# Index scores pair by pair inside the projection tiles of a fused transformer kernel, instead of a stage of their own

## The chip, the cores and the metric

One core of a Trainium2 chip runs the whole program. The metric is the device time in microseconds (us) of one execution, lower is better. The engines are TensorE (PE: matmuls; PEld: its weight loads), VectorE (DVE), ScalarE (ACT), GpSimd (POOL) and SyncE (SP), which issues the loads of the weights.

## The reference, cut to what matters

The program computes two models one after the other. The change lies in the first one: two layers, 528 positions (16 learned ones and 512 of the sequence), width 1024. Each layer projects the normed input into many parts. Three of them, `qi`, `ki` and `wi`, score the keys for each query (the indexer), and only the 128 best keys of a query are attended to:

```python
for l in range(DEPTH):                       # 2 layers
    n = rms_norm(h, mix_norm_g[l])
    proj = jnp.einsum("btd,de->bte", n, w_in[l])
    q, k, v, qi, ki, wi, xr, yg, cv, gt = _split_cols(proj)
    q = rotary(rms_norm(q...)); k = rotary(rms_norm(k...))
    qi = rotary(qi...)          # 8 index heads of 64
    ki = rotary(ki...)          # one of 64
    attn = dsa_attention(q, k, v, qi, ki, wi * idx_scale)
    ...
# in dsa_attention, per block of queries
logits = jnp.einsum("bqhd,bsd->bqhs", qib, ki)
iscore = jnp.einsum("bqhs,bqh->bqs", jax.nn.relu(logits), wib)
iscore = jnp.where(admiss[None], iscore, -jnp.inf)
_, sel = lax.top_k(iscore, topk)
```

Behind the projections of q and k come the projections of the convolution branch (`cv`, a gated linear unit) and of the recurrence (`xr`, `yg`), which don't need the scores.

## The kernel before, in words

All weights stream through in 548 blocks of 128 x 1024 fp32. SyncE loads a block, GpSimd splits it into a high and a low part (`whi`, L466, and `wlo`, L468) as soon as TensorE has finished the block two before it (two slots), and TensorE makes one output tile of 128 rows of it. A tile is 8 groups of products (hi with hi, hi with lo, lo with hi: L493, L494, L496), over 528 columns in two halves of 264, or over 512. Tiles go to two accumulators in turn (`acc`, slots 0 and 1), and a tile waits for `evac` of its slot: the reader of the tile two before must be done. Two more pairs of banks, `aux[0]` and `aux[1]`, take everything else.

Each engine's program is written out by hand and runs in its order, with semaphores between the engines; no scheduler moves anything. In a layer (`proj`, L594) TensorE makes 4 tiles of v, ki and wi, 3 of qi, and 10 of the phase `kq`: 2 of k (e = 0, 1) and 8 of q (e = 2 to 9). For each of the ten, ScalarE squares the tile into `tsq` (L1108), copies it with its gain into `tqg` (L1111, which frees the accumulator) and swaps its halves into `tsw` (L1114, L1115); TensorE sums the squares (`qk_sum`, L577, one tile later; for q into single columns of `aux[1]`, second bank, from column `QSUM` = 128 on); VectorE rotates it (`turn`, L1830 to L1833, with a reciprocal of 3.45 us for each of the two k tiles). Behind e = 3 ScalarE copies the transposed `wi` out of `aux[1]` (L1120, `wi_copied`).

Then comes `index(l)` (L633), a stage of its own on three engines. For each of 4 query tiles i (W = 144, 272, 400, 528 admissible keys) and each of 8 heads, TensorE multiplies 64 rows of qi with 64 rows of ki in fp32 into `aux[head % 2]`; even heads lie on rows 0 to 63, odd heads on rows 64 to 127. ScalarE takes the relu into `tsq[head % 2]` (L1141), VectorE adds it, times the head's weight, onto the score in `mask` (L1877 for the first head, L1880 for the others). TensorE may write a bank pair again when the relu two heads before is done (`ix_relu`), ScalarE may write a `tsq` again when its add is done (`ix_acc`).

Behind it TensorE makes the 16 tiles of the convolution's projections. ScalarE takes the sigmoid of the even ones (slot 0) into `csg` (L1214), VectorE multiplies the odd ones (slot 1) with it into `cu` (L1982, which frees slot 1), and after each such product runs one eighth of `choose`: the search for the 128 best scores of each query (MAX8 and MATCH_REPLACE8, L1892, L1893). In layer 0 VectorE first runs `decay_rates` (L2419 to L2438), some 32 very small operations on constants of the recurrence, with one exp of ScalarE (L1649) in between.

## Time and profile before

| | us |
|---|---|
| median of 3 runs | 3664.69 (3662.44 to 3665.59) |
| profiled execution | 3665.75 |
| its span in the trace | 3663.9 |
| TensorE busy in it | 3530.1 (96%) |
| mean granted TensorE clock | 0.976 |

The runs lie 3 us apart. The page and the answers of the trace are of the one profiled execution; all its times count from the start of its span. "Busy" of TensorE is by records of pipelined matmuls, whose ends are modelled, so they overlap: what a matmul costs is read from one start to the next. PEclk is the granted clock as a share of 2.4 GHz.

### The profile page before, as it was taken

The numbers are of one execution on the slowest core, as the hardware profiler recorded it, in microseconds if no ns is written. First come the engines' busy times: TensorE is split into PE (matmuls) and PEld (weight loads), VectorE is DVE, ScalarE is ACT, GpSimd is POOL, SyncE is SP. The second block draws the span as 40 slices with busy tenths as digits, with TensorE's granted clock in tenths as the row PEclk, the third lists the DMA queues.
The fourth block names the chain that finished last, engine by engine and source line by source line (L and its number), as shares of the span: only waits on it lengthen the run. The fifth ranks groups of instructions, "written<-read, shape, count | busy, mean of one in ns | idle before, by whom it ended". The sixth has DMA issues, their size and how long they took to land.

```text
span 3663.9 us, 49850 instructions
## 1 busy us (share of the span) xinstructions
PE 3530.1 (96%) x20100; PEld 3036.7 (83%) x20100; DVE 2347.0 (64%) x2977; ACT 988.4 (27%) x1711; POOL 2040.9 (56%) x1100
## 2 busy tenths in 40 slices
PE   7999899999999999989999999999999999999997
PEld 7899788999999879867778788877887875688886
DVE  6677898577833666788857873387336755743335
ACT  4405542222110340454231111011003444322201
POOL 4355334465666535533556776677665552466664
PEclk9799999999999989999999999999999999999999
DMA  3122111222322312211222342333235341222332
GB/s 134 51 85 78 53 47 64 72 90 94 128 90 100 109 58 76 79 54 53 75 81 93 133 146 98 103 132 135 97 103 189 142 148 63 87 97 92 103 103 69
DMA packets 96898, 348.30 MB, mean 95 GB/s; under 512 B 10848, under 2 KB 13152, under 8 KB 93664
## 3 DMA queue, kind: packets, MB, share of 16 engines
q1 hardware_dynamic: 80064, 289.44, 23.8%
q10 hardware_dynamic: 16672, 56.70, 4.1%
q8 instruction: 101, 1.65, 0.2%
q14 instruction: 61, 0.50, 0.0%
HBM read 322.32 MB, written 23.79 MB: 94 GB/s over the span
## 4 chain that ended last, share of the span: by engine, by line
PE 46%; DVE 8%; ACT 2%; issue 1%; DMA 1%; POOL 0%; ACTq 0%; DVEq 0%; POOLq 0%
PE acc L493 13%; PE acc L494 13%; PE acc L496 13%; DVE ptmp L2177 1%; PE aux L795 1%; PE acc L743 1%; PE acc L824 1%; PE aux L803 1%; DVE pcp L2177 1%; PE aux L882 0%; PE aux L714 0%; PE aux L729 0%; DMA m<-kept_m 0%; DVE fpr L1758 0%; DVE alo L1760 0%
## 5 line engine op out<-in xcount | busy, mean ns | idle before, releaser
L466 POOL TENSOR_SCALAR whi<-raw 128x1024 fp32r<-128x1024 f32 x548 | 619.2, 1130 | 1549.2 <-PE acc L496 1528.0
L468 POOL TENSOR_TENSOR wlo<-raw,whi 128x1024 fp32r<-128x1024 f32 x548 | 1421.8, 2594 | 45.7
L493 PE MATMUL acc<-nhi,whi 128*128 128x512 f32 (+1 forms) x2776 | 951.9, 351 | 26.6 <-DVE nlo L1718 15.0
L494 PE MATMUL acc<-nlo,whi 128*128 128x512 f32 (+1 forms) x2776 | 944.7, 349 | 0.0
L496 PE MATMUL acc<-nhi,wlo 128*128 128x512 f32 (+1 forms) x2776 | 866.9, 347 | 0.0
L493 PEld LDWEIGHTS acc<-nhi,whi 128*128 128x128 f32 x2776 | 524.4, 189 | 110.8 <-issue 21.5
L494 PEld LDWEIGHTS acc<-nlo,whi 128*128 128x128 f32 x2776 | 524.2, 189 | 68.9
L493 PE MATMUL acc<-bhi,whi 128*128 128x264 f32 (+1 forms) x1864 | 555.4, 314 | 13.3 <-ACT tqg L1099 5.5
L494 PE MATMUL acc<-blo,whi 128*128 128x264 f32 (+1 forms) x1864 | 543.6, 308 | 0.0
L496 PEld LDWEIGHTS acc<-nhi,wlo 128*128 128x128 f32 x2776 | 485.8, 189 | 67.2
L496 PE MATMUL acc<-bhi,wlo 128*128 128x264 f32 (+1 forms) x1864 | 448.3, 307 | 0.0
L493 PEld LDWEIGHTS acc<-bhi,whi 128*128 128x128 f32 x1864 | 355.5, 191 | 33.7 <-ACT tqg L1099 6.8
L494 PEld LDWEIGHTS acc<-blo,whi 128*128 128x128 f32 x1864 | 355.5, 191 | 15.4
L496 PEld LDWEIGHTS acc<-bhi,wlo 128*128 128x128 f32 x1864 | 304.9, 191 | 14.9
L494 PE MATMUL acc<-alo,whi 128*128 128x512 f32 (+1 forms) x880 | 300.2, 349 | 0.0
L493 PE MATMUL acc<-ahi,whi 128*128 128x512 f32 (+1 forms) x880 | 300.1, 349 | 0.0
L496 PE MATMUL acc<-ahi,wlo 128*128 128x512 f32 (+1 forms) x880 | 279.8, 351 | 0.0
L1755 DVE TENSOR_TENSOR fpr<-acc,frs 128x512 f32<-128x512 f32 (+1 forms) x88 | 61.2, 696 | 236.2 <-PE acc L496 231.2
L1760 DVE TENSOR_TENSOR alo<-fpr,ahi 128x512 fp32r<-128x512 f32 (+2 forms) x88 | 165.0, 1875 | 66.6 <-ACT ahi L1027 66.6
L1027 ACT ACTIVATE ahi<-fpr 128x512 fp32r<-128x512 f32 (+2 forms) x88 | 56.0, 636 | 559.7 <-DVE fpr L1758 559.7
L494 PEld LDWEIGHTS acc<-alo,whi 128*128 128x128 f32 x880 | 165.6, 188 | 23.5
L493 PEld LDWEIGHTS acc<-ahi,whi 128*128 128x128 f32 x880 | 165.7, 188 | 22.1
(372 smaller groups left out, 4735.8 us busy)
## 6 DMA issues: line engine op xcount, KB each, us to landing
raw<-in_w SPq DMA_DIRECT2D x548, 512.0 KB, 3.3
kept_cp<-pcp ACTq DMA_DIRECT2D x4, 1280.0 KB, 6.5
cp<-kept_cp ACTq DMA_DIRECT2D x4, 1280.0 KB, 10.0
kept_ap<-pap ACTq DMA_DIRECT2D x4, 1024.0 KB, 4.0
kept_cs<-pcs ACTq DMA_DIRECT2D x4, 1024.0 KB, 6.4
ap__144<-kept_ap ACTq DMA_DIRECT2D x4, 1024.0 KB, 6.4
cs__155<-kept_cs ACTq DMA_DIRECT2D x4, 1024.0 KB, 6.6
merge_gates<-gout ACTq DMA_DIRECT2D x16, 256.0 KB, 3.1
```

Of the source, the lines that this page charges most:

```text
L466: pool.tensor_scalar(hi, w, 1.0, 0.0, ALU.mult, ALU.add).then_inc(sem("w_hi"), 1)
L468: pool.tensor_tensor(lo, w, hi.bitcast(F32), ALU.subtract).then_inc(sem("w_split"), 1)
L493: pe.matmul(acc[s][:, f, 0:TH], hi, xh[:, f * TH:(f + 1) * TH], start=a, stop=False)
L494: pe.matmul(acc[s][:, f, 0:TH], hi, xl[:, f * TH:(f + 1) * TH], start=False, stop=False)
L496: m = pe.matmul(acc[s][:, f, 0:TH], lo, xh[:, f * TH:(f + 1) * TH], start=False, stop=z)
L743: m = pe.matmul(out, v[0:w, c, (hh // 4) * P:(hh // 4 + 1) * P], pts[0:w, c, 0:r], start=c == 0, stop=c == len(ps) - 1)
L795: pe.matmul(aux[0][:, 0, :], q2[rows, hh // 2, i * P:(i + 1) * P], k2[rows, hh // 2, :], start=True, stop=True).then_inc(sem("na_s"), 1)
L803: m = pe.transpose(aux[1][:, 0, c * P:(c + 1) * P], na_scores(j)[:, c * P:(c + 1) * P], ident[:, :])
L1027: act.activation(out[:, :, 0:T], fpr[:, 0:T].unsqueeze(1), ACT.Copy).then_inc(sem("ff_hi"), 1)
L1755: dve.tensor_tensor(halves(fpr[:, 0:T], T), accv(s1, T), rs, ALU.mult).then_inc(evac[s1], 1)
L1760: dve.tensor_tensor(lo[:, :, 0:T], fpr[:, 0:T].unsqueeze(1), hi[:, :, 0:T].bitcast(F32), ALU.subtract)\
L2177: tt = lambda o_, a, b_, op: then(dve.tensor_tensor(o_, a, b_, op))
```

## The change

The stage is dissolved. `index(l, pair)` now does one pair of heads (even and odd) of a query tile, 16 pairs in a layer, on each of the three engines, and the pairs stand inside other work:

- In TensorE's order, each q tile from e = 4 on (`IX_TILE`) is cut in the middle: four of its eight groups of products, a pair, the other four groups; then the norm sum of the tile before, then a second pair. Six tiles take pairs 0 to 11. The convolution's first two tiles are cut in the same way and take pairs 12 to 15; the norm sum of the last q tile stands ahead of pair 12.
- ScalarE's relus stand ahead of the square of the same tile (first pair) and between the copy and the swap (second pair); VectorE's adds of both pairs stand ahead of the rotation of the tile.
- The relus go to a buffer of their own, `ixr`, no longer to `tsq`.
- The widest scores (528) are cut into 264 and 264 columns instead of 512 and 16, and the column sums move to column 272 (`QSUM`), clear of them.
- ScalarE's first sigmoid (`conv_gate(l, 0)`) stands between pairs 12 and 13, its square roots of the norms (`std_q`) behind pair 15, and in layer 0 the exp of `decay_rates` behind that. VectorE's `decay_rates` stands behind pair 15's adds as before.
- The first pair waits in addition for `k_std`: `aux[0]` must have been read.

```diff
@@ constants
-QSUM = 128
+QSUM = 272
...
+IX_TILE = 4
+IX_CUT = [META + P * (i + 1) for i in range(NQT - 1)] + [T1 // 2]
...
+        ixr, o1 = at("ixr", [P, 2, T1], end_rnn_w)
@@ TensorE
+            def parted_tile(ph, i, rhs, T, between):
+
+                s, b = ph.slot(i), ph.block(i)
+                if ph.nth(i):
+                    pe.wait_ge(evac[s], ph.nth(i))
+                pe.wait_ge(sem("w_split"), b + 1)
+                products(s, b % 2, 0, KD // 2, rhs, T, True, False)
+                between()
+                products(s, b % 2, KD // 2, KD // 2, rhs, T, False, True, w0=KD // 2).then_inc(pe_block, 1)
...
                 for e in range(10):
-                    tile(kq, e, normed if e < KV else mine, T1 if e < KV else T)
+                    if e < IX_TILE:
+                        tile(kq, e, normed if e < KV else mine, T1 if e < KV else T)
+                    else:
+                        parted_tile(kq, e, mine, T, lambda: index(l, 2 * (e - IX_TILE)))
                     if e:
                         qk_sum(l, e - 1)
                     if e == 1:
                         turn_wi()
-
-            def index(l):
...
+                    if e >= IX_TILE:
+                        index(l, 2 * (e - IX_TILE) + 1)
+
+            def index(l, pair):
+
+                i = pair // (IXH // 2)
+                W, cut = META + P * (i + 1), IX_CUT[i]
+                if pair == 0:
+                    pe.wait_ge(sem("pj_done"), 15 * l + 5)
+                    pe.wait_ge(sem("wi_copied"), l + 1)
+                    pe.wait_ge(sem("k_std"), KV * (l + 1))
+                for z in range(2):
+                    it = l * NQT * IXH + 2 * pair + z
+                    if it >= 2:
+                        pe.wait_ge(sem("ix_relu"), it - 1)
+                    rows = slice(64 * z, 64 * z + 64)
+                    lhs = qi[rows, pair % (IXH // 2), META + i * P:META + (i + 1) * P]
+                    m = pe.matmul(aux[z][:, 0, 0:cut], lhs, ki[rows, 0:cut], start=True, stop=True)
+                    if W > cut:
+                        m = pe.matmul(aux[z][:, 1, 0:W - cut], lhs, ki[rows, cut:W], start=True, stop=True)
+                    m.then_inc(sem("ix_logit"), 1)
...
-                index(l)
-                for n in range(16):
-                    tile(AT[f"conv{l}"], n, R(bhi, blo, T1), T1)
+                conv, normed = AT[f"conv{l}"], R(bhi, blo, T1)
+
+                def last_sum():
+                    qk_sum(l, 9)
+                    index(l, 12)
+
+                parted_tile(conv, 0, normed, T1, last_sum)
+                index(l, 13)
+                parted_tile(conv, 1, normed, T1, lambda: index(l, 14))
+                index(l, 15)
+                for n in range(2, 16):
+                    tile(conv, n, normed, T1)
@@ ScalarE
+                for z in range(2):
+                    it = l * NQT * IXH + 2 * pair + z
+                    act.wait_ge(sem("ix_logit"), it + 1)
+                    if it >= 2:
+                        act.wait_ge(sem("ix_acc"), it - 1)
+                    if W > cut:
+                        act.activation(halves(ixr[:, z, 0:W], W), aux[z][:, :, 0:cut], ACT.Relu).then_inc(sem("ix_relu"), 1)
+                    else:
+                        act.activation(ixr[:, z, 0:W], aux[z][:, 0, 0:W], ACT.Relu).then_inc(sem("ix_relu"), 1)
...
-                index(l)
+                index(l, 12)
+                conv_gate(l, 0)
+                for pair in range(13, 16):
+                    index(l, pair)
+                std_q(l)
                 if l == 0:
                     act.wait_ge(sem("lam_abs"), 1)
                     act.activation(prep[:, 1, :], prep[:, 0, :], ACT.Exp, scale=-1.0).then_inc(sem("lam_exp"), 1)
-                conv_gates(l)
+                for n in range(1, KD):
+                    conv_gate(l, n)
@@ VectorE
                 for e in range(HEADS):
+                    if KV + e >= IX_TILE:
+                        index(l, 2 * (KV + e - IX_TILE))
+                        index(l, 2 * (KV + e - IX_TILE) + 1)
                     turn(7 + e, q[:, e, LO[l]:], LT[l], LO[l], 0)
...
-                index(l)
+                for pair in range(12, 16):
+                    index(l, pair)
+                dve.wait_ge(sem("ix_acc"), (l + 1) * NQT * IXH)
                 if l == 0:
                     decay_rates()
                 conv_inputs(l)
```

How it moves instructions. TensorE's row in layer 0 before, from the end of the last q tile (`acc`) through the norm sums (`aux<-ones,tsq`) into the stage of index scores (`aux<-ki,qi`, a count for the heads):

```order
L493 MATMUL acc<-bhi,whi 128x264
L494 MATMUL acc<-blo,whi 128x264
L496 MATMUL acc<-bhi,wlo 128x264 x2
L589 MATMUL aux<-ones,tsq 128x1 x4
L589 MATMUL aux<-ones,tsq 16x1
L644 MATMUL aux<-ki,qi 128x144 x2
L589 MATMUL aux<-ones,tsq 128x1 x4
L589 MATMUL aux<-ones,tsq 16x1
L644 MATMUL aux<-ki,qi 128x144 x6
L644 MATMUL aux<-ki,qi 128x272 x8
L644 MATMUL aux<-ki,qi 128x400 x8
L644 MATMUL aux<-ki,qi 128x512
```

TensorE's row now, in the middle of the first cut q tile (e = 4), around pair 0:

```order
L498 MATMUL acc<-blo,whi 128x264
L500 MATMUL acc<-bhi,wlo 128x264 x2
L666 MATMUL aux<-ki,qi 128x144 x2
L497 MATMUL acc<-bhi,whi 128x264
L498 MATMUL acc<-blo,whi 128x264
```

and at that tile's end, around the norm sum and pair 1:

```order
L500 MATMUL acc<-bhi,wlo 128x264 x2
L603 MATMUL aux<-ones,tsq 128x1 x4
L603 MATMUL aux<-ones,tsq 16x1
L666 MATMUL aux<-ki,qi 128x144 x2
L497 MATMUL acc<-bhi,whi 128x264
```

The run of score matmuls is gone; two heads at a time stand between products that don't need them.

VectorE's row before, at the end of the last rotation (`q<-tqg,tsw`) in layer 0: all adds in a run, then `decay_rates` (`prep`).

```order
L1830 TENSOR_TENSOR tqg<-tqg,rope 128x528
L1831 TENSOR_TENSOR tsw<-tsw,rope 128x528
L1833 TENSOR_TENSOR q<-tqg,tsw 128x528
L1877 TENSOR_SCALAR mask<-tsq,wi 128x144
L1880 SCALAR_TENSOR_TENSOR mask<-tsq,wi,mask 128x144 x7
L1877 TENSOR_SCALAR mask<-tsq,wi 128x272
L1880 SCALAR_TENSOR_TENSOR mask<-tsq,wi,mask 128x272 x7
L1877 TENSOR_SCALAR mask<-tsq,wi 128x400
L1880 SCALAR_TENSOR_TENSOR mask<-tsq,wi,mask 128x400 x7
L1877 TENSOR_SCALAR mask<-tsq,wi 128x528
L1880 SCALAR_TENSOR_TENSOR mask<-tsq,wi,mask 128x528 x7
L2419 COPY prep<-par 128x8 x2
```

VectorE's row now, at the same place:

```order
L1920 SCALAR_TENSOR_TENSOR mask<-ixr,wi,mask 128x400 x4
L1867 TENSOR_TENSOR tqg<-tqg,rope 128x528
L1868 TENSOR_TENSOR tsw<-tsw,rope 128x528
L1870 TENSOR_TENSOR q<-tqg,tsw 128x528
L1917 TENSOR_SCALAR mask<-ixr,wi 128x528
L1920 SCALAR_TENSOR_TENSOR mask<-ixr,wi,mask 128x528 x7
L2458 COPY prep<-par 128x8 x2
```

Four adds (two pairs) stand ahead of each rotation, and only the adds of the widest query tile are left between the last rotation and `decay_rates`. They now wait for pairs that TensorE makes inside and behind the convolution's first two tiles.

## Rows read from the trace of the kernel before

**Rows 1.** The page's part 1: busy time, share of the span, instructions.
```profile
PE 3530.1 (96%) x20100; PEld 3036.7 (83%) x20100; DVE 2347.0 (64%) x2977; ACT 988.4 (27%) x1711; POOL 2040.9 (56%) x1100
```
**Rows 2.** By stretch: length, busy time of each engine (instructions), PEclk, DMA share, GB/s.
```profile
101.34:143.16 41.82, 41.82 (x350) 41.60 (x348) 23.99 (x23) 15.44 (x26) 21.47 (x13) 1.00 0.24 76
143.16:178.99 35.83, 31.91 (x93) 21.06 (x91) 18.80 (x33) 14.71 (x34) 2.64 (x2) 0.53 0.05 15
178.99:182.67 3.68, 3.68 (x17) 3.68 (x17) 2.83 (x9) 3.04 (x7) 0.00 (x0) 0.50 0.01 2
...
1302.66:1341.50 38.84, 38.84 (x194) 32.49 (x193) 24.50 (x23) 15.00 (x26) 21.40 (x13) 1.00 0.25 82
1341.51:1377.43 35.92, 31.88 (x90) 21.06 (x89) 18.82 (x33) 14.83 (x34) 2.77 (x2) 0.52 0.05 15
1377.43:1380.75 3.32, 3.32 (x16) 3.32 (x16) 1.60 (x3) 2.09 (x4) 0.00 (x0) 0.50 0.02 5
```
**Rows 3.** TensorE's timeline, score stage: start, length, line, tiles, count [idle <-releaser].
```profile
143.16 0.52 PE L644 MATMUL aux<-ki,qi 64*128 64x144 f32 x4
143.61 1.19 PE L589 MATMUL aux<-ones,tsq 128*128 128x1 f32 x10
...
173.23 2.57 PE L644 MATMUL aux<-ki,qi 64*128 64x512 f32 x4 [0.20 <-ACT tsq L1141]
```
**Rows 4.** TensorE's timeline at full clock: fp32 sums of squares, a tile's start.
```profile
86.30 1.05 PE L583 MATMUL aux<-tsq,ones 128*128 128x264 f32 x4
...
87.65 0.39 PE L493 MATMUL acc<-bhi,whi 128*128 128x264 f32 x1
87.88 0.28 PE L494 MATMUL acc<-blo,whi 128*128 128x264 f32 x1
```
**Rows 5.** ScalarE's timeline around the copy of wi, in layer 0 and in layer 1.
```profile
104.70 0.70 ACT L1111 ACTIVATE tqg<-acc,par 128x528 f32<-128x528 f32 x1 [3.56 <-DVE k L1838]
...
106.76 0.20 ACT L1120 ACTIVATE wi<-aux 128x32 f32<-128x32 f32 x1
...
1308.26 0.20 ACT L1120 ACTIVATE wi<-aux 128x32 f32<-128x32 f32 x1
```
**Rows 6.** Groups by shape, 143 to 180 us: busy, mean ns | idle before.
```profile
L1880 DVE SCALAR_TENSOR_TENSOR mask<-tsq,wi,mask 128x528 f32<-128x528 f32 x6 | 4.6, 768 | 4.7 <-ACT tsq L1141 4.4
L1141 ACT ACTIVATE tsq<-aux 128x528 f32<-128x528 f32 x8 | 4.5, 608 | 7.6 <-PE aux L646 7.6
```
**Rows 7.** Timelines of VectorE and of GpSimd behind a q tile's end.
```profile
137.95 1.58 DVE L1830 TENSOR_TENSOR tqg<-tqg,rope 128x528 f32<-128x528 f32 x1 [3.91 <-ACT tsw L1115]
139.56 0.71 DVE L1831 TENSOR_TENSOR tsw<-tsw,rope 128x528 f32<-128x528 f32 x1
...
136.57 2.40 POOL L468 TENSOR_TENSOR wlo<-raw,whi 128x1024 fp32r<-128x1024 f32 x1
```
**Rows 8.** VectorE's timeline: decay_rates of layer 0 and the first product cu.
```profile
180.91 0.38 DVE L2419 COPY prep<-par 128x8 f32<-128x8 f32 x2
...
186.67 3.74 DVE L2436 TENSOR_SCALAR hba<-par 128x8 f32<-128x8 f32 x4
...
192.72 0.71 DVE L1982 TENSOR_TENSOR cu<-acc,csg 128x528 f32<-128x528 f32 x1 [1.88 <-issue]
```
**Rows 9.** ScalarE's timeline and a stretch (columns as in rows 2) of the convolution.
```profile
210.28 0.61 ACT L1214 ACTIVATE csg<-acc 128x528 f32<-128x528 f32 x1 [11.13 <-PE acc L496]
...
200.00:240.00 40.00, 40.00 (x329) 40.00 (x328) 32.08 (x87) 1.84 (x3) 23.06 (x14) 1.00 0.28 92
```
**Rows 10.** TensorE alone: two waits, each with its slow stretch: length, busy, PEclk, DMA.
```profile
292.47:294.51 2.04, 0.01 (x2) 1.00 0.19 76
295.30:298.70 3.40, 3.40 (x12) 0.50 0.27 82
...
1588.95:1595.29 6.34, 0.00 (x1) 0.77 0.18 55
1592.40:1599.20 6.80, 3.91 (x9) 0.50 0.24 80
```

More of the change, by code:

```diff
@@ L1104, in proj @@
                     T = T1 if e < KV else LT[l]
+                    if e >= IX_TILE:
+                        index(l, 2 * (e - IX_TILE))
                     block_done(kq.block(e) + 1)
@@ L1112, in proj @@
                        .then_inc(evac[s], 1)
+                    if e >= IX_TILE:
+                        index(l, 2 * (e - IX_TILE) + 1)
                     act.wait_ge(evac[s], kq.nth(e) + 1)
@@ L1128, in std_q, with index @@
                 act.activation(qstd[:, 0:NQT], sums[:, 0:NQT], ACT.Sqrt, bias=EPS, scale=1.0 / HD).then_inc(sem("q_std"), 1)
-            def index(l):
-                for i in range(NQT):
-                    W = META + P * (i + 1)
-                    for hh in range(IXH):
-                        it = (l * NQT + i) * IXH + hh
-                        act.wait_ge(sem("ix_logit"), it + 1)
-                        if hh >= 2 or i:
-                            act.wait_ge(sem("ix_acc"), it - 1)
-                        src = aux[hh % 2][:, :, :].rearrange("p a b -> p (a b)")[:, 0:W]
-                        if it == l * NQT * IXH:
-                            act.wait_ge(sem("qk_sum"), 10 * (l + 1))
-                        act.activation(tsq[:, hh % 2, 0:W], src, ACT.Relu).then_inc(sem("ix_relu"), 1)
-                std_q(l)
+            def index(l, pair):
+                i = pair // (IXH // 2)
+                W, cut = META + P * (i + 1), IX_CUT[i]
+                for z in range(2):
[7 more added lines that the diff above has]
+                        act.activation(ixr[:, z, 0:W], aux[z][:, 0, 0:W], ACT.Relu).then_inc(sem("ix_relu"), 1)
             def exps(l, j):
@@ L1206, in rnn, with conv_gate @@
                 part(7)
-            def conv_gates(l):
+            def conv_gate(l, n):
                 ph = AT[f"conv{l}"]
-                for n in range(KD):
-                    block_done(ph.block(2 * n) + 1)
-                    if n:
-                        act.wait_ge(evac[1], ph.nth(2 * n - 1) + 1)
-                    act.activation(halves(csg[:, :], T1), accv(0, T1), ACT.Sigmoid).then_inc(evac[0], 1)
+                block_done(ph.block(2 * n) + 1)
+                if n:
+                    act.wait_ge(evac[1], ph.nth(2 * n - 1) + 1)
+                act.activation(halves(csg[:, :], T1), accv(0, T1), ACT.Sigmoid).then_inc(evac[0], 1)
             def att_split(l):
@@ L1865, in query_scales, with index @@
                 then(dve.reciprocal(qrs[:, 0:NQT], qstd[:, 0:NQT]))
-            def index(l):
-                dve.wait_ge(sem("wi_copied"), l + 1)
-                for i in range(NQT):
-                    W = META + P * (i + 1)
-                    sc = mask[:, i, 0:W]
-                    for hh in range(IXH):
-                        it = (l * NQT + i) * IXH + hh
-                        r, w = tsq[:, hh % 2, 0:W], wi[:, i, hh:hh + 1]
-                        dve.wait_ge(sem("ix_relu"), it + 1)
-                        if hh == 0:
-                            dve.tensor_scalar(sc, r, w, None, ALU.mult).then_inc(sem("ix_acc"), 1)
-                        else:
-                            dve.wait_ge(sem("ix_acc"), it)
-                            dve.scalar_tensor_tensor(sc, r, w, sc, ALU.mult, ALU.add).then_inc(sem("ix_acc"), 1)
-                dve.wait_ge(sem("ix_acc"), (l + 1) * NQT * IXH)
+            def index(l, pair):
+                i = pair // (IXH // 2)
+                sc = mask[:, i, 0:META + P * (i + 1)]
+                if pair == 0:
+                    dve.wait_ge(sem("wi_copied"), l + 1)
+                for z in range(2):
+                    it, hh = l * NQT * IXH + 2 * pair + z, 2 * (pair % (IXH // 2)) + z
+                    r, w = ixr[:, z, 0:META + P * (i + 1)], wi[:, i, hh:hh + 1]
+                    dve.wait_ge(sem("ix_relu"), it + 1)
+                    if hh == 0:
+                        dve.tensor_scalar(sc, r, w, None, ALU.mult).then_inc(sem("ix_acc"), 1)
+                    else:
+                        dve.wait_ge(sem("ix_acc"), it)
+                        dve.scalar_tensor_tensor(sc, r, w, sc, ALU.mult, ALU.add).then_inc(sem("ix_acc"), 1)
             def choose(l, n):
```

18 lines of the change are left out of this document (2 added, 16 removed).

## Prediction

> **What bounds the kernel now.** I read the page's busy shares first: TensorE matmuls are busy for 3530.1 of 3663.9 us, VectorE for 64%, ScalarE for 27% [rows 1]. TensorE is the path nearly everywhere, so a change is worth what it takes out of TensorE's own row of work, waits and slow clock. The table by stage shows where the change works. The index scores of the first layer fill 35.83 us and those of the second 35.92 us, at a mean granted clock of 0.53 and 0.52; the query projections ahead of them run at 1.00 [rows 2]. The clock also stays at its lower level (0.50, that is 1.2 of 2.4 GHz) for the first 3.68 and 3.32 us of the convolution's first tile [rows 2]. TensorE's timeline shows why the stage is long. The first pair of heads, still at full clock, is over in 0.45 us (143.16 to 143.61); later pairs each wait for ScalarE's relu of the pair before, and one of the widest keeps TensorE for 2.57 us at half clock [rows 3]. It is a loop of matmul, relu and weighted add with nothing beside it.
>
> **What is taken out.** From 143.16 to 178.99 is 35.83 us, in which one norm sum of 1.1 us stays (it moves into the convolution's first tile): 34.7 us go. The slow head of the convolution, 3.68 us at half rate, did 1.84 us of work, so 1.8 us more go. Layer 0: 36.5 us. Layer 1: 35.92 - 1.0 + 1.66 = 36.6 us. Together **73.1 us**.
>
> **What is put in: 16 pairs of matmuls a layer, in TensorE's row.** The two heads of a pair stand on different halves of the rows and run side by side. At full clock four fp32 matmuls of 264 columns take 1.05 us with the tail of the last [rows 4], 0.22 to 0.24 each, so four of 512 columns at half clock would take 3.7 us one after the other; they took 2.57 [rows 3], so they overlap. So a pair of 144 columns costs 0.45 us (seen), 272 columns 2 x 0.23 + 0.1 = 0.56, 400 columns 2 x 0.34 + 0.1 = 0.78, and 528 columns, now cut 264 and 264, 4 x 0.22 + 0.1 = 1.0; four of each make 11.2 us. A tile that starts again after such a group loses 0.11 us (first matmul 0.23 us to the next [rows 4] instead of the 0.12 that a tile of 5.87 us [rows 9] gives each of its 48), 16 times: 1.8 us. That is 13.0 us a layer, **26.0 us** in all. From below it is bounded by the columns alone, some 10 us a layer. From above, each way in and out of the two-halves arrangement could cost the tail of a matmul: a record lasts 0.28 us where the next starts after 0.12 [rows 4, 9], so 0.16 us, 32 times, 5.1 us instead of the 1.8.
>
> On this the Trainium skill has a rule that speaks against the change: "TensorEngine Tiling (Array Packing)", section Key Properties, says that changing the tiling mode drains TensorE. In the row at 143.16 the norm sum behind the pair starts 0.45 us after the pair did, which leaves no room for a full drain beside the work; by the rule taken at its worst the sum would be that of the rival "drains" below.
>
> **Waits that the change adds.** Three.
>
> (a) The first pair needs wi, the weights of the heads, which ScalarE copies at 106.76 to 106.96, held up by the key's rotation on VectorE (its copy at 104.70 waited 3.56 us for k) [rows 5]. Nothing ahead of that point is changed. TensorE begins the tile at 101.34 [rows 2] and would reach the pair half a tile (2.98 us) later, at 104.3, and wait until 107.05: **2.7 us**. In layer 1 it is 1302.66 + 2.84 = 1305.50 against 1308.5: **3.0 us** [rows 2, 5]. Before, the copy had 36 us of cover.
>
> (b) Pair on pair. TensorE's next pair needs the relus of the last one, about 3.1 us later in its row (half a tile, or half a tile and a norm sum). The widest relu takes 0.61 us, the widest add 0.77 [rows 6]. But VectorE's adds now meet GpSimd, which in the old stage stood idle. A VectorE operation with two SBUF operands that starts during one of GpSimd's splits of the weights lasts until that is over: the rotation at 137.95 took 1.58 us instead of 0.71, ending when the split that began at 136.57 did [rows 7]. The Trainium skill says the same ("SBUF — State Buffer", the exclusive lock on the shared port pair); the trace agrees. After the change the second pair of each tile is added from the split's end, 3.65 us behind the tile's end. VectorE's work in a tile is then the wait of about 2.1 us, four adds of 1.7 to 2.7 us and the rotation of 2.2 us, at most 7.0 of the tile's 8.1 to 8.8 us. The relus are done 1.8 to 2.4 us before TensorE wants them: **0 us**, and ScalarE (27% busy, one or two table loads more, each while it waits anyway) hides the rest.
>
> (c) The accumulator of the convolution's second tile. Call T the end of that tile on TensorE. The last pair follows it, its relus end at T + 1.8, its first add meets the split (T + 0.1 to T + 3.7) and ends at T + 4.4, the second at T + 5.2. In layer 0 VectorE has decay_rates next: from 180.91 to 190.84, 9.9 us, with 3.0 us of stops for GpSimd in it (four small constants take 3.74 us instead of 0.7, where GpSimd splits the weights behind the first tile) [rows 8]. It meets the next split again, begun at T + 7.0, so it is over at T + 15.2. Only then comes the product cu, 0.71 us, which frees the accumulator (evac1): T + 16.1. TensorE has the pair (1.1 us) and tile 2 (5.87 us: two tiles lie between ScalarE's sigmoids, 11.13 + 0.61 [rows 9]) and wants the accumulator for tile 3 at T + 7.0. It waits **9.1 us**. In the old order this work lay under the first two tiles and ended 1.88 us before cu could run [rows 8], so it was free; the change takes the cover. Bounds: without meeting GpSimd 4.9 us, with two more stops 11.5 us. In layer 1 there is no decay_rates: cu ends at T + 6.0, before 7.0, **0 us**. From then on VectorE catches up: it is busy for 32.08 of 40 us there, 9.4 of the 11.74 us of two tiles [rows 9]; the end of the convolution and the recurrence behind it see it as before.
>
> **The clock.** A wait of TensorE of 2.04 us is followed by 3.4 us at 0.50; one of 6.34 us lowers the clock within it, 6.8 us long and 3.9 us past its end [rows 10]. Work done in those stretches takes twice as long: 1.7 us lost behind each wait of (a) (none, if the clock holds), 2.0 us behind (c) if the same 3.9 us fall behind it, 3.4 if all 6.8 do, say 2.8. Together **6.2 us**. In the tiles with pairs I expect 1.00.
>
> **Sum.** 73.1 - 26.0 - 5.7 - 9.1 - 6.2 = **26.1 us**: some 7 in layer 0 and 19 in layer 1. The profiled execution took 3665.75 us (span 3663.9), 1.06 above the median of the three runs, 3664.69. So 3639.6 for a profiled execution, and **3638.6** as a median.
>
> **Rivals.**
> - Light stall: the adds and decay_rates slip between the splits and the clock stays up behind the short waits. (c) is 4.9 us and the clock costs 2 us: 8.4 us less, 3630. For: the meeting times are worked out, not seen. Against: operations as small as the constants did stop [rows 8].
> - Drains: the dearer boundary, 5.1 us a layer instead of 1.8, 6.6 us more, 3645. For: the rule of the page. Against: the seen 0.45 us.
> - Deep stall: decay_rates stops at a second split, or the low clock behind it stretches tile 3 so that tile 5 waits too: 2.4 + 4 us, 3645 to 3651.
> - Pair by pair: the old loop comes back inside the tiles, each pair waiting for the relu before it, whose add waits for GpSimd. It decides once the margin of about 2 us is used up; at 0.8 us lost at each of 32 pairs the gain is gone, 3664.
> - Slower: the half clock comes with the pairs themselves. The old stage was at 0.53, with TensorE's records nearly continuous [rows 2, 3]; if the fp32 matmuls on half of the rows hold the clock down rather than the gaps between them, the eight tiles that now hold pairs, about 47 us a layer, run at half: 94 us more, 3733. It decides from 52 us of low clock in all (half of it is 26). Against: the clock was still full in the first pair and fell only once the waits had begun.
>
> **Chances.** The forecast 0.66, its own range 3632 to 3645; light stall 0.13; drains and deep stall 0.12; pair by pair 0.04; slower 0.05. The range of 8 in 10 takes the forecast, most of the light stall and most of the two dear cases: 3628 to 3649. A measurement of this kernel tells 0.2%, 7.3 us, from no change. Faster by more: 0.91; within: 0.03; slower by more: 0.06.
>
> **What would show it.** Right: no stretch of index scores alone; TensorE's granted clock near 1.00 from the fourth query tile to the convolution's second but for some 3.4 us behind two waits for wi; one wait of about 9 us for cu ahead of the convolution's fourth tile in layer 0, none there in layer 1; layer 1 gaining over twice what layer 0 does; VectorE's add behind each tile's end at 1.8 to 2.6 us instead of 0.4 to 0.8. Wrong: waits of TensorE for ixr relus (pair by pair), a granted clock of 0.5 across the q tiles, pairs of 400 columns that take over 1 us at full clock, or no wait ahead of the fourth tile.

## The result and the profile after

The changed kernel takes 3640.18 us (median of 4 runs, 3638.83 to 3640.98), the kernel before 3664.24 beside it (4 runs). The ratio is 0.9934, with a 95% interval of 0.992 to 0.9947: 24.1 us faster. The profiled execution took 3640.31 us with a span of 3638.2, 25.7 under the span before. Of these 25.7, 1.7 us arise ahead of the first changed matmul, where the kernels are the same, in part by a stretch at half clock near 57 us that only the profiled execution before had (its clock is 0.72 from 56 to 62 us, after it is 1.00).

The page's part 1 of the changed kernel answers to [rows 1]: TensorE's busy time fell from 3530.1 to 3496.3 us. Part of that is no work saved: the same matmuls are shorter at the upper clock.

```profile
PE 3496.3 (96%) x20100; PEld 3005.5 (83%) x20100; DVE 2357.7 (65%) x2977; ACT 991.6 (27%) x1715; POOL 2039.8 (56%) x1100
```

By stretch, TensorE alone (length, busy time with its instructions, granted clock, DMA share, GB/s), against [rows 2]: in each layer from the start of kq tile 4, the first with a pair in it, until behind the last pair; then the slow stretches of layer 0 in them (layer 1 has one, 3.4 us from 1300.6).

```profile
99.60:178.46 78.86, 76.35 (x584) 0.98 0.18 61
1293.44:1367.10 73.66, 70.81 (x402) 0.98 0.17 58
...
105.88:109.29 3.41, 3.41 (x16) 0.51 0.00 0
181.00:191.20 10.20, 4.16 (x19) 0.50 0.13 51
```

No stretch of scores at 0.53 is left; the tiles with the pairs in them run at 0.98, and what is missing to 1.00 is one stretch of 3.4 us behind the first pair in each layer. (The first stretch holds the convolution's third tile too, which ends at 178.46, where the long stop begins; the last pair ends at 172.34. In layer 1 it ends at 1364.10, 3 us ahead of the end of the stretch.)

TensorE's timeline (start, length, line, tiles, count, idle before) shows a pair of each width, with the tile's matmul that follows, and the one long stop:

```profile
105.31 0.52 PE L666 MATMUL aux<-ki,qi 64*128 64x144 f32 x4 [2.51 <-DVE q L1870]
...
122.92 0.73 PE L666 MATMUL aux<-ki,qi 64*128 64x272 f32 x4
123.58 0.39 PE L497 MATMUL acc<-bhi,whi 128*128 128x264 f32 x1
123.81 0.28 PE L498 MATMUL acc<-blo,whi 128*128 128x264 f32 x1
...
139.85 0.94 PE L666 MATMUL aux<-ki,qi 64*128 64x400 f32 x4
...
158.56 0.72 PE L666 MATMUL aux<-ki,qi 64*128 64x264 f32 x4
159.11 0.62 PE L668 MATMUL aux<-ki,qi 64*128 64x264 f32 x4
159.66 0.39 PE L497 MATMUL acc<-bhi,whi 128*128 128x264 f32 x1
...
187.04 0.59 PE L497 MATMUL acc<-bhi,whi 128*128 128x264 f32 x1 [8.58 <-DVE cu L2021]
```

From a pair's first matmul to the tile's next it is 0.44, 0.66, 0.88 and 1.10 us, and the tile's first matmul takes 0.23 to its next (123.58 to 123.81). Ahead of a pair in the middle of a tile 0.09 us are lost too: the last matmul of the half takes 0.21 to the pair instead of 0.12. The pair of 144 columns costs what the very first one cost in [rows 3], at full clock, and no pair but the first of a layer waits.

ScalarE's timeline, against [rows 5]: the copy of wi (L1153) comes 1.75 us earlier than before, as the tile itself does (the 1.7 us from above), and TensorE's first pair starts 0.1 us behind it. TensorE's row names q as releaser; the copy is the last thing that the pair needed, as the first experiment shows.

```profile
102.95 0.70 ACT L1142 ACTIVATE tqg<-acc,par 128x528 f32<-128x528 f32 x1 [3.56 <-DVE k L1875]
...
105.01 0.20 ACT L1153 ACTIVATE wi<-aux 128x32 f32<-128x32 f32 x1
```

VectorE's timeline from the last pairs of layer 0 to the product cu, against [rows 6 to 8], and below it GpSimd's, with the splits of the weights beside it:

```profile
168.85 1.64 DVE L1920 SCALAR_TENSOR_TENSOR mask<-ixr,wi,mask 128x528 f32<-128x528 f32 x2 [0.94 <-ACT ixr L1173]
173.08 3.29 DVE L1920 SCALAR_TENSOR_TENSOR mask<-ixr,wi,mask 128x528 f32<-128x528 f32 x2 [2.59 <-ACT ixr L1173]
176.41 0.38 DVE L2458 COPY prep<-par 128x8 f32<-128x8 f32 x2
...
178.61 1.01 DVE L2468 TENSOR_TENSOR prep<-prep 128x16 f32<-128x16 f32 x1
...
179.86 2.19 DVE L2468 TENSOR_TENSOR prep<-prep 128x16 f32<-128x16 f32 x1
...
186.28 0.71 DVE L2021 TENSOR_TENSOR cu<-acc,csg 128x528 f32<-128x528 f32 x1
```

```profile
172.53 2.40 POOL L472 TENSOR_TENSOR wlo<-raw,whi 128x1024 fp32r<-128x1024 f32 x1
...
178.55 1.05 POOL L470 TENSOR_SCALAR whi<-raw 128x1024 fp32r<-128x1024 f32 x1 [3.62 <-PE acc L500]
179.68 2.34 POOL L472 TENSOR_TENSOR wlo<-raw,whi 128x1024 fp32r<-128x1024 f32 x1
```

The adds of the last pair, of which the first starts during the split at 172.53, take 3.29 us together and not the 1.64 of the pair before. The first ends at 175.50, 0.56 us behind the split: it stood until the split was over and then still had most of its own work to do. Then come the decay rates, 9.8 us, with two more stops, 1.01 and 2.19 us for an operation of 0.17, which end with GpSimd's two operations at 178.55 and 179.68. Only then comes cu.

### The profile page after: what moved, and what is told of

Same layout as the page of the kernel before. It is cut to its first block, busy times and chain, and to the rows that moved or that the text cites. A ratio compares the mean times of both kernels' runs of the same rounds, so it can differ in the third digit from the quotient of the medians.

```text
span 3638.2 us, 49855 instructions
## 1 busy us (share of the span) xinstructions
PE 3496.3 (96%) x20100; PEld 3005.5 (83%) x20100; DVE 2357.7 (65%) x2977; ACT 991.6 (27%) x1715; POOL 2039.8 (56%) x1100
## 4 chain that ended last, share of the span: by engine, by line
PE 46%; DVE 8%; ACT 2%; issue 1%; DMA 1%; POOL 0%; ACTq 0%; DVEq 0%; POOLq 0%
PE acc L497 14%; PE acc L500 13%; PE acc L498 13%; DVE ptmp L2216 1%; PE aux L815 1%; PE acc L763 1%; PE acc L844 1%; PE aux L823 1%; ACT us L1550 1%; DVE pcp L2216 1%; DVE ru L1978 0%; PE aux L734 0%; PE aux L749 0%; PE aux L902 0%; DMA m<-kept_m 0%
## 5 line engine op out<-in xcount | busy, mean ns | idle before, releaser
L497 PE MATMUL acc<-bhi,whi 128*128 128x264 f32 (+1 forms) x1864 | 556.8, 315 | 24.9 <-DVE cu L2021 8.6
L497 PEld LDWEIGHTS acc<-bhi,whi 128*128 128x128 f32 x1864 | 355.2, 191 | 57.1 <-issue 10.2
L498 PEld LDWEIGHTS acc<-blo,whi 128*128 128x128 f32 x1864 | 354.9, 190 | 14.9
L1086 ACT ACTIVATE fsq<-h 128x528 f32<-128x528 f32 x56 | 36.2, 646 | 546.6 <-DVE h L1824 332.1
```

The lines of the kernel that those rows point to most:

```text
L497: pe.matmul(acc[s][:, f, 0:TH], hi, xh[:, f * TH:(f + 1) * TH], start=a, stop=False)
L498: pe.matmul(acc[s][:, f, 0:TH], hi, xl[:, f * TH:(f + 1) * TH], start=False, stop=False)
```

## The experiments

The theory: the gain is the stage that is gone, with its waits and its half clock; what is lost of it are three waits, each the price of one position in a queue, and the slow stretches behind them. Rivals: that the buffers carry the gain, that boundaries or the order of the matmuls matter, or that the waits have other causes. All comparisons are with 3640.2 for the changed kernel; the kernel before stood at 3664.7 to 3665.3 beside these runs, against 3664.2, so that some 0.5 to 1 us of such a difference is not the kernel's.

### The copy of wi one tile earlier

```
-                    if e == 3:
+                    if e == 2:
                         act.wait_ge(sem("wi_turned"), l + 1)
```

> One edit to the changed kernel: ScalarE copies the turned score weights (wi) behind the swap of q/k tile 2 instead of tile 3, in both layers. Nothing is left out. My theory: in the profile of the changed kernel TensorE stood for 2.5 us (102.80 to 105.31) and 2.85 us (1296.48 to 1299.33) before the first pair, because the copy of wi came to the head of ScalarE's queue late; each stop was followed by a stretch of 3.4 us at half clock, worth 1.7 us each. With the copy a tile earlier both stops and both slow stretches go: 2.5 + 2.85 + 3.4 = 8.8 us, so about 3631.4 us beside 3640.2 of the changed kernel. Rival A: the first pair's start is held by something else as well (its tile, the adds), and only a part comes back: 0 to 4 us, 3636 to 3640. Rival B: the slow stretches are not due to the stops but come up anyway somewhere near: 5.4 us, 3634.8.

Measured: 3632.46 us (5 runs), ratio to before 0.9913 (0.99 to 0.9927); 7.7 us less than the changed kernel. TensorE's timeline and ScalarE's:

```profile
103.71 0.52 PE L666 MATMUL aux<-ki,qi 64*128 64x144 f32 x4
```

```profile
103.94 0.70 ACT L1142 ACTIVATE tqg<-acc,par 128x528 f32<-128x528 f32 x1 [3.56 <-DVE k L1875]
```

The first pair starts without a wait, at 103.71, before ScalarE's evacuation of the tile behind which the copy stood, at 103.94. The slow stretches behind the pairs are gone in both layers. So the wait was the copy's place in the queue. But a smaller one takes its place, at the third pair. TensorE's rows of it in both layers, and the relu of the second pair that it waits for:

```profile
111.82 0.98 PE L666 MATMUL aux<-ki,qi 64*128 64x144 f32 x4
...
1302.21 0.98 PE L666 MATMUL aux<-ki,qi 64*128 64x144 f32 x4 [0.54 <-ACT ixr L1175]
```

```profile
111.47 0.29 ACT L1175 ACTIVATE ixr<-aux 128x144 f32<-128x144 f32 x1 [2.89 <-DVE mask L1917]
```

That pair keeps TensorE for 0.91 us instead of 0.45, in layer 1 behind a wait of 0.54. The relu stood for the first add, which came late on VectorE. In the changed kernel the long wait for wi had hidden this. It is 0.5 us in layer 0 and 1.0 in layer 1, and so most of what is missing to the 8.8 us expected: by the traces layer 0 gained 3.6 us and layer 1 3.4.

### The decay rates spread among the pairs' adds

```
                     if KV + e >= IX_TILE:
                         index(l, 2 * (KV + e - IX_TILE))
+                        if l == 0 and KV + e != IX_TILE + 1:
+                            next(rates, None)
                         index(l, 2 * (KV + e - IX_TILE) + 1)
...
-                if l == 0:
-                    decay_rates()
```

> One edit to the changed kernel: the decay rates of layer 0 (VectorE's work between the last pair's adds and the layer's first evacuation of a convolution tile) are cut in six pieces and put between the two pairs' adds of the query tiles 4 and 6 to 9, the last piece ahead of pair 13; ScalarE's exp for them goes ahead to tile 5. Nothing is left out. My theory: the stop of 8.6 us in layer 0 (178.46 to 187.04, TensorE waiting for VectorE's evacuation of a convolution tile) is caused by the decay rates standing in VectorE's queue at 176.4 to 186.2, and the half clock of 10.2 us from 181.0 by that stop; 7 us of those 10.2 lie within the stop and about 4 us of it behind, worth about 2.1 us. With the rates spread: 8.6 + 2.1 = 10.7 us less, about 3629.5 us beside 3640.2. Rival A: the stop has another cause, which the queue's order only hides (ScalarE's square, a queue of evacuations behind the pairs): it shrinks only by a part, 3634 to 3640. Rival B: the pieces delay the adds of the pairs, and through the two buffers the next pair's matmuls: small stops at 5 tiles come instead, and 3 to 5 us of the gain are given back, 3633 to 3635.

Measured: 3625.28 us (4 runs), ratio 0.9889 (0.9874 to 0.9904); 14.9 us less. VectorE's timeline: an operation of one of the pieces, and cu behind the last adds.

```profile
136.11 1.03 DVE L2473 TENSOR_SCALAR prep<-prep 128x16 f32<-128x16 f32 x1
...
173.83 3.29 DVE L1922 SCALAR_TENSOR_TENSOR mask<-ixr,wi,mask 128x528 f32<-128x528 f32 x2 [2.59 <-ACT ixr L1176]
...
177.28 0.71 DVE L2023 TENSOR_TENSOR cu<-acc,csg 128x528 f32<-128x528 f32 x1
```

The same operations, the stop at 136.11 too, now cost TensorE nothing: cu starts 0.2 us behind the last add, and no wait for it is left. Matmul by matmul, the traces of the two kernels move apart by 10.7 us around 187 us, the 8.6 of the wait and 2.1 of clock that the theory had. That the time fell by 4 us more has its largest part, 2.4 us, some 1270 us later, in layer 1, where the edit changes nothing. TensorE's wait for the first taps there, in the changed kernel (us in total, times, longest):

```profile
PE aux L685 <- DVE ru L1978: 4.5, 1, 4.5
```

With the rates spread the same wait is 2.1 us long (1454.33 to 1456.40). The reason shows in VectorE's three taps and GpSimd's split, first of the changed kernel, then of the kernel with both edits (below), where the wait is 2.1 us as well:

```profile
1463.21 5.10 DVE L1978 SCALAR_TENSOR_TENSOR ru<-rx,par,ru 128x528 f32<-128x528 f32 x3
```

```profile
1465.08 2.67 POOL L472 TENSOR_TENSOR wlo<-raw,whi 128x1024 fp32r<-128x1024 f32 x1
```

```profile
1445.24 3.03 DVE L1980 SCALAR_TENSOR_TENSOR ru<-rx,par,ru 128x528 f32<-128x528 f32 x3
```

```profile
1447.80 2.69 POOL L472 TENSOR_TENSOR wlo<-raw,whi 128x1024 fp32r<-128x1024 f32 x1
```

Where the split starts 1.9 us behind the first of the three taps, they take 5.10 us; where it starts 2.6 us behind, 3.03. The third tap decides: it starts at 1465.58, 0.5 us behind the split's start, and takes 2.73 us, or at 1446.85, 0.95 us ahead of it, and takes 1.42. A shift of 0.7 us between two engines is worth 2.1 us to VectorE and 2.4 to TensorE. These 2.4 us are luck, not an effect of the spread rates as such; they are in the result of the kernel with both edits too. With the copy of wi alone moved the wait was 4.5 us as before; what makes the shift was not tested.

### Both

> The two edits together (wi copied one tile earlier, the decay rates spread among the pairs' adds). Nothing is left out. My theory, by which the two stops are separate mechanisms that add: 8.8 + 10.7 = 19.5 us, about 3620.7 us beside 3640.2 of the changed kernel. Rival: time saved on TensorE's queue in the projections is taken back by a later wait (the gates' stops of 2.05 and 4.5 us at 283 and 1464 us grow by it, or those of a DMA), so that the two together give less than the sum of the two apart: 3624 to 3632.

Measured: 3618.2 us (4 runs), ratio 0.9873 (0.9858 to 0.9888); 22.0 us less than the changed kernel, where the two edits gave 7.7 and 14.9 alone. The two waits are separate causes and add up. The third pair still loses the 0.5 and 1.0 us of the first experiment, and the 2.4 us at the taps of the second are in the 22.0, so that the two moves by themselves gave some 19.6, beside 19.5 expected. (In the trace the taps' wait of layer 1 is 2.1 us long.) From 98 to 170 us, the stretch of the pairs in layer 0, the granted clock is 1.00 (and so it is in layer 1):

```profile
98.00:170.00 72.00, 72.00 (x561) 1.00 0.18 62
```

### The stage kept, with the new buffers and cuts

```
-                        parted_tile(kq, e, mine, T, lambda: index(l, 2 * (e - IX_TILE)))
+                    tile(kq, e, normed if e < KV else mine, T1 if e < KV else T)
...
+                for pair in range(16):
+                    index(l, pair)
+                    if pair == 0:
+                        qk_sum(l, 9)
+                for n in range(16):
                     tile(conv, n, normed, T1)
```

> One part of the change alone: the buffers of their own for the relus and the cuts of the rows are kept as in the changed kernel, but the 16 pairs of each layer stand again in a stage of their own behind the last query projection, and the tiles are whole. Nothing is left out. My theory is that the gain comes from the place alone: in a stage of their own each pair waits for relu and adds, whatever the buffers. Then the time is that of the kernel before within 3 us: about 3662 us (3659 to 3667). Rival: the buffers of their own carry a good part of the gain, since relu and adds no longer exclude each other there: 8 us or more of the 24 come with the stage kept, 3656 us or less.

Measured: 3662.93 us (10 runs), ratio 0.9993 (0.9983 to 1.0002), not to be told from before. The stretch of the scores in layer 0, all engines in the columns of [rows 2]:

```profile
144.84:180.60 35.76, 31.77 (x91) 19.36 (x92) 20.53 (x37) 15.33 (x36) 1.22 (x1) 0.52 0.04 16
```

Own buffers without the new place give nothing: the stage has its old length and its old clock.

### Both pairs behind the tile

```
-                        parted_tile(kq, e, mine, T, lambda: index(l, 2 * (e - IX_TILE)))
+                        tile(kq, e, mine, T)
...
+                        index(l, 2 * (e - IX_TILE))
                         index(l, 2 * (e - IX_TILE) + 1)
```

> One part of the change undone: the eight tiles that had a pair in their middle are whole again, and both pairs stand one behind the other at the tile's end (ScalarE and VectorE take them in the same order). Nothing is left out. My theory: a pair directly behind a pair must wait for the relus of the first, whose buffers in the banks it overwrites. From the first pair's end that is a relu of 0.5 to 0.8 us for each half and its hand-overs, so 0.5 to 1.0 us of waiting at each of the 16 second pairs, 8 to 16 us in all; against it stand the mid-tile restarts of TensorE that go, 16 times 0.1 to 0.2 us. About 3649 us beside 3640.2 of the changed kernel (3644 to 3656). Rival: the relu is ready within the run of matmuls of the same pair, the stops are hidden, and only the restarts go: 3637 to 3640.

Measured: 3650.94 us (7 runs), ratio 0.9963 (0.9951 to 0.9974); 10.8 us more than the changed kernel. TensorE's timeline at a pair behind a pair:

```profile
125.11 0.73 PE L667 MATMUL aux<-ki,qi 64*128 64x272 f32 x4
126.32 1.01 PE L667 MATMUL aux<-ki,qi 64*128 64x272 f32 x4 [0.48 <-ACT ixr L1177]
```

The second pair waits for the relu of the first, and its two heads start apart, since each waits for its own: two pairs take 2.15 us instead of 2 x 0.66. Over the widths it is 0.6, 0.8, 1.05 and 1.2 us, twice each in a layer: some 15 us, less the mid-tile restarts (3 to 4 us), and a stretch at the lower clock comes back in each layer (0.70 from 156.5 to 160, 0.83 from 1330 to 1340). So 3 us of tile between two pairs are worth more than the restart that they cost.

### The scores twice, head by head and by turns

```
+                    for _ in range(2):
+                        m = pe.matmul(aux[z][:, 0, 0:cut], lhs, ki[rows, 0:cut], start=True, stop=True)
```

> Each score matmul of the changed kernel is issued twice in a row, into the same place with the same operands, so that the output stays the same; nothing is left out. This prices the pairs' matmuls by themselves where they now stand. My theory of the sum: they cost 11.2 us a layer (22.4 in both) at full clock and the restarts around them 1.8 us a layer; the second issue adds the first part alone: about 22 us, 3662 us beside 3640.2. Rival A: the boundaries between the pairs and the tile (TensorE changing from 128 rows to 64 and back) are the dear part and the matmuls of the two row halves overlap: less than 16 us more, under 3656. Rival B: the longer pairs delay the relus and adds and make new stops: over 26 us more, above 3666.

Measured: 3662.65 us (10 runs), ratio 0.9993 (0.9984 to 1.0003); 22.5 us more. The number is the theory's, its parts are not. Doubled pairs of 144, 272 and 400 columns take 0.70, 1.12 and 1.55 us (0.25, 0.46 and 0.68 more), those of 528 columns 2.97, 1.87 more instead of 0.88:

```profile
163.99 0.71 PE L667 MATMUL aux<-ki,qi 64*128 64x264 f32 x2
164.54 0.61 PE L669 MATMUL aux<-ki,qi 64*128 64x264 f32 x2
164.98 0.72 PE L667 MATMUL aux<-ki,qi 64*128 64x264 f32 x4
165.43 0.71 PE L669 MATMUL aux<-ki,qi 64*128 64x264 f32 x4
165.98 0.60 PE L667 MATMUL aux<-ki,qi 64*128 64x264 f32 x2
166.43 0.61 PE L669 MATMUL aux<-ki,qi 64*128 64x264 f32 x2
166.96 0.39 PE L497 MATMUL acc<-bhi,whi 128*128 128x264 f32 x1
```

The first four records are one head alone, the middle eight both, the last four the other alone. By the widths the doubling costs TensorE some 26 us in the two layers, and 1.3 us of that come back in the wait for cu (7.3 us). The rest of the difference to 22.5 was not traced, so that the hit on 22 is in part luck. The order was then tested by itself:

```
-                for z in range(2):
+                for n in range(4):
+                    z = n % 2
```

> Each score matmul again twice, the same work as in the run with the scores doubled, but the two heads take turns: head 0, head 1, head 0, head 1 instead of twice head 0 and then twice head 1. Nothing is left out. In that run a doubled pair of 144, 272 and 400 columns took 0.25, 0.46 and 0.68 us more than a single one, as two heads side by side do; a pair of 528 columns took 1.87 us more instead of 0.88, and the second head's matmuls began beside the first's only when the first had four records left. Theory A: the heads go side by side only if the second's matmuls stand at most some four records behind the first's in TensorE's queue; by turns they do, and the widest pairs fall to 0.88 us more each, 8 x 0.99 = 7.9 us less than 3662.7: about 3655 us. Rival: the widest pairs are limited by something else (two banks written at a time); the order changes nothing, 3661 to 3664.

Measured: 3654.76 us (7 runs), ratio 0.9973 (0.9962 to 0.9985); 7.9 us less. TensorE's timeline of the same pair:

```profile
164.16 0.72 PE L667 MATMUL aux<-ki,qi 64*128 64x264 f32 x4
164.71 0.62 PE L669 MATMUL aux<-ki,qi 64*128 64x264 f32 x4
165.15 0.71 PE L667 MATMUL aux<-ki,qi 64*128 64x264 f32 x4
165.59 0.72 PE L669 MATMUL aux<-ki,qi 64*128 64x264 f32 x4
166.24 0.39 PE L497 MATMUL acc<-bhi,whi 128*128 128x264 f32 x1
```

The widest pairs fall to 2.08 us, from 2.97, eight times 0.89: 7.1 of the 7.9 us. It was the order in the queue.

### One relu buffer

```
-                    if it >= 2:
-                        act.wait_ge(sem("ix_acc"), it - 1)
+                    if it >= 1:
+                        act.wait_ge(sem("ix_acc"), it)
...
+                        act.activation(halves(ixr[:, 0, 0:W], W), aux[z][:, :, 0:cut], ACT.Relu).then_inc(sem("ix_relu"), 1)
```

> The changed kernel with one of the two relu buffers alone: both relus of a pair write the same one, so that the second waits for the first's add, and each pair's first relu for the last pair's second add. Nothing is left out. My theory: inside the tiles a pair has 5.8 us until the next, and relu, add, relu, add take about 3.5 us in a row, 5.1 us where the first add stands still for GpSimd's split; so nothing of it reaches TensorE but perhaps at the pairs behind the tiles' ends of layer 0's last two tiles: 0 to 1 us, 3640 to 3641 us. Rival: ScalarE's evacuation of the query tile stands behind the second relu and comes late for TensorE's next tile but one: 1 us at each of 12 tiles, 3650 us or more.

Measured: 3640.23 us (4 runs), ratio 0.9932 (0.9916 to 0.9949): the same as with two. In the trace one pair of each layer is late by most of a microsecond, though. In layer 0, ScalarE's timeline and TensorE's:

```profile
168.19 0.61 ACT L1173 ACTIVATE ixr<-aux 128x528 f32<-128x528 f32 x1 [2.42 <-DVE mask L1920]
```

```profile
168.05 0.71 PE L666 MATMUL aux<-ki,qi 64*128 64x264 f32 x2
...
168.86 0.71 PE L666 MATMUL aux<-ki,qi 64*128 64x264 f32 x2
```

The relu of the pair before stood 2.42 us for an add that GpSimd's split held up, and the second head of pair 14 could start only behind that relu, at 168.86: 1.89 us instead of 1.10, and the wait for cu became 9.6 us. Layer 1 shows 2.08 us at the same pair, and five earlier pairs there are late by 0.05 to 0.31. In the runs this does not show, and where the traces win it back was not looked into. With two buffers TensorE came to the next pair 2.4 us or more after the first relu of the last one was over; with one buffer the 2.4 us of an add's stop are enough to use that up.

### Cuts of 512 and 16

```
-IX_CUT = [META + P * (i + 1) for i in range(NQT - 1)] + [T1 // 2]
+IX_CUT = [META + P * (i + 1) for i in range(NQT - 1)] + [512]
```

> One part of the change undone: the rows of 528 columns are cut 512 and 16 again, as in the kernel before, instead of 264 and 264, in the eight widest pairs; relu reads the two banks as one row. Nothing is left out. My theory: the columns are the same and the number of matmuls too, so TensorE's row is the same to 0.1 us a pair: 3640.2 with 1 us to either side. Rival: a matmul of 16 columns costs far more than its columns, as the sums of one column do, 0.12 us each, and with two of them per head 0.2 us a pair come on top, 2 us: 3642.

Measured: 3641.04 us (4 runs), ratio 0.9936 (0.9919 to 0.9952). A pair of 528 columns takes 1.19 us instead of 1.10, eight times 0.09: 0.7 us. The even cut is worth that much at most.

### Both, and the first taps ahead of the choice's end

```
                 taps(0)
+                for _ in rest_of_mask:
+                    pass
+                dve.sem_inc(sem("mask_done"), 1)
```

> The two edits that were tried together (wi copied a tile earlier, decay rates spread) and a third: the last round of the top-k choice of the last row block and the mask's end (3.4 us of VectorE's work in each layer) go behind the first taps of the recurrent branch, which TensorE's first gates wait for. Nothing is left out. My theory: the stops of TensorE before the gates, 2.0 and 2.1 us in that kernel, go, since VectorE has 3.5 us of idle time right behind those taps: 4.1 us less than 3618.2, about 3614. Rival A: the taps are bound by the evacuation of their own tile and not by the choice before them: only 0.2 to 1 us of each stop goes, 3617 us. Rival B: GpSimd's work, which lies differently beside the taps, holds them by 2 us or more as in layer 1 of the changed kernel (4.5 us there): no gain, 3618 to 3621.

Measured: 3613.67 us (4 runs), ratio 0.9863 (0.9847 to 0.988); 4.5 us less than both edits without it, and the fastest kernel here, 26.5 us under the changed one. VectorE's timeline in layer 1, and what TensorE still waits for there:

```profile
1438.36 4.38 DVE L1983 SCALAR_TENSOR_TENSOR ru<-rx,par,ru 128x528 f32<-128x528 f32 x3
```

```profile
PE aux L685 <- DVE ru L1983: 0.6, 1, 0.6
```

The taps meet a split in this order (4.38 us), and it costs only 0.6 us, since they start earlier. In layer 0 no wait is left there. The 0.5 us at the third pair of layer 1 stay.

## Why the prediction was right

It said 3638.6 (3628 to 3649); the result is 3640.2. The terms, in the order of its sum, with what the trace of the changed kernel and the runs give:

- **Taken out, 73.1.** The stage is gone. The kernel with the stage put back is as slow as the one before. With the measured terms below the 36.5 and 36.6 give the measured gain of each layer to 0.3 us: 36.5 - 13.9 - 2.5 - 8.6 - 3.8 = 7.7 against 7.6, and 36.6 - 14.5 - 2.85 - 1.7 = 17.55 against 17.3.
- **Put in, 26.0; measured 28.4.** This is the term that was too small. From the start of kq tile 4 to the end of the last pair, without the wait for wi and the 1.7 us of its slow stretch, TensorE takes 172.34 - 99.60 - 2.5 - 1.7 = 68.5 us in layer 0 against 54.7 for the same tiles and the norm sum before (41.82 + 1.1 + 2 x 5.87 [rows 2, 3, 9]), so 13.9 for the pairs, and 66.1 against 51.6 in layer 1, 14.5. What was mis-sized is the pair of 272 columns and more: 0.1 us was added to the columns for start and boundary, and it is 0.2 (0.66, 0.88, 1.10 where 0.56, 0.78 and 1.0 stood; only 0.45 was seen). That makes 12.3 a layer for 11.2. The restarts came near their 1.8 us (1.6 and 2.2 are left for them), but not as they were counted, 16 times 0.11: a tile that starts behind a norm sum takes 0.23 us to its second matmul anyway [rows 4], so only the nine pairs a layer that stand straight behind a tile's matmuls cost one, 0.09 us ahead and 0.11 behind each. The columns alone, priced by the scores doubled by turns, are 9.4 us a layer, so that starts, changes and restarts together cost 4.5 and 5.1. The rival "drains" put 16.3 us a layer, which the 13.9 and 14.5 do not reach; whether TensorE drains in part at a change is not shown, and the 0.2 us beside the columns leave room for it.
- **(a) The wait for wi, 2.7 and 3.0; measured 2.51 and 2.85.** With the copy earlier the wait is gone; 0.5 and 1.0 us come in its place at the third pair.
- **(b) Pair on pair, 0; measured 0.** An add behind a tile's end takes 2.4 us, as said. The relus are done at least 2.4 us before TensorE wants them, where 1.8 to 2.4 was said. That the margin comes from the 3 us of tile between two pairs is shown by the kernel with the tiles uncut (10.8 us dearer). One reading in this step was wrong: the rotation at 137.95 did not end with the split (138.97), but 0.56 us later, at 139.53 [rows 7]. The times of (c) held all the same, since there an add's own time was put behind the split's end (T + 4.4; it ended at T + 4.3).
- **(c) The wait for cu, 9.1; measured 8.58**, with the decay rates as its cause, since it goes when they are spread. None in layer 1. From the second tile's end, T = 171.2, the rates begin at T + 5.2 as forecast and cu is over at T + 15.8 (16.1 forecast); TensorE wants the accumulator at T + 7.2 (7.0). The 3.0 us of stops in the rates came as two, 0.8 and 2.0, in other operations than before.
- **The clock, 6.2; measured 5.5.** 3.4 us at 0.50 behind each wait of (a), and 10.2 us from 181.0 around (c), of which 4.2 lie behind it and cost 2.1, where 2.8 was taken. The rival "slower", by which the matmuls on half of the rows hold the clock down, is refuted: the clock is 1.00 in all tiles with pairs once the waits are gone, and the stage put back runs at 0.52 with the same matmuls.

The sum with these numbers is 73.1 - 28.4 - 5.4 - 8.6 - 5.5 = 25.2 us. That the forecast came so near has some luck in it: the pairs cost 2.4 us more than said, the waits and the clock 1.5 us less. The mechanism, each wait with its place and its size, was as forecast. The traces show it by layer: from kq tile 4 to the first gates of the recurrence layer 0 gained 7.6 us (7 forecast) and layer 1 17.3 (19 forecast), 24.9 together, and the medians differ by 24.1 us. The 7.6 of layer 0 is a near hit by the same offset; in layer 1 the dearer pairs show. The light stall was refuted by the two stops in the decay rates (8.58 us and not 4.9), the deep one since no further tile waits.

What the prediction did not ask is how cheaply the three waits could be had back: three small groups of instructions moved in the queues of ScalarE and VectorE gave another 22.0 us beside the 24.1, of which 2.4 are the lucky taps of layer 1.

## What to carry to other kernels

A loop of small steps between engines costs TensorE its waits and then its clock; the same matmuls put pair by pair between halves of large tiles cost some 0.3 us a pair beside their columns (14 us a layer, where the stage took 36), if the time between two of them is longer than the way through relu and add. What to look for in such a move is everything that lay under the old stage for nothing: here the copy of the weights and the decay rates had 36 and 12 us of cover, and became TensorE's waits; two moves in the queues gave 22.0 us, nearly as much again as the change had. Name each such step, and where TensorE would next ask for it, before the stage goes. And look again when a wait is gone: here a smaller one had stood hidden behind it.

## What the runs showed of the hardware

- Two heads on different halves of the rows ran side by side from the start where four records of the one stood ahead of the other in the queue (158.56, and the doubled narrow pairs: 0.70 us for 0.45). With eight records of one head ahead the other began when four were left (164.98), and by turns the same work took 2.08 us instead of 2.97. Nothing between four and eight was tried.
- A VectorE operation of 16 elements a row stands for GpSimd's weight split too, until it is over: 1.01, 2.19 and 1.03 us instead of 0.17. Both of GpSimd's operations do it; the stops end with them (179.62 and 182.05, beside 179.60 and 182.02). An add or a rotation of 528 elements ends 0.56 us behind the split (175.50 beside 174.93, 139.53 beside 138.97).
- A shift of 0.7 us between VectorE and GpSimd, 1270 us behind the place of an edit, put one operation of VectorE ahead of a split instead of behind its start and was worth over 2 us: a difference of that size between two kernels is not to be put down to an edit without looking where it arises.
- A pair on half of the rows costs 0.2 us beside its columns at every width from 144 to 528, and in the middle of a tile another 0.2 us in the tile's own matmuls. What of it is the change between half and whole rows was not separated.
